# Bias rows built on all 128 partitions and stored from ScalarE's queue, recurrent blocks overlapped by one, 16 modulation chunks moved into the attention stage

## What is computed

```python
mod = silu(c) @ w_ada + b_ada                 # 6 x 1024: sh1, sc1, ga1, sh2, sc2, ga2
xn = rms_norm(h, g_mix) * (1 + sc1) + sh1
q, k, v, qi, ki, wi, xr, yr, gate_a, gate_b = split(xn @ w_in + b_in)

# attention: of each row the 128 best by the index score, a bias by distance
score = sum_h wi_h * relu(qi_h . ki); sel = top_k(causal(score), 128)
attn = softmax(q . k[sel] / 8 + rel_bias[t5_bucket(t - sel)]) @ v[sel]

# recurrent branch, 8 blocks of 128 channels
xr = causal_dwconv(xr, conv_w, conv_b)        # 4 taps
r, i = sigmoid(xr @ w_rg + b_rg), sigmoid(xr @ w_ig + b_ig)
log_a = -8 * r * softplus(-lam); a = exp(log_a)
u = xr * i * sqrt(-expm1(2 * log_a))
rnn = scan(h_t = a_t * h_{t-1} + u_t) * gelu(yr)

merged = sigmoid(gate_a) * (attn @ w_o_attn) + sigmoid(gate_b) * (rnn @ w_o_rnn)
h = h + ga1 * (merged @ w_out)                # then a gated FFN with sh2, sc2, ga2
```

## Time and profile before

| | us |
|---|---|
| median of 3 runs | 1988.12 |
| lowest, highest | 1985.82, 1991.65 |
| the profiled execution's own time | 1989.59 |
| span of its trace | 1987.5 |
| mean granted TensorE clock | 0.961 of full speed |
| PE busy | 1828.1 (92%) |
| POOL, DVE, ACT busy | 1277.8, 959.8, 660.6 |

### The profile page before, as it was taken

The page is one execution under the profiler, slowest core; times in us unless marked ns, Lnnn a source line. Parts: engine busy times, 40 slices in busy tenths (PEclk is TensorE's granted clock), DMA queues, the critical chain, the costliest instruction groups (busy, mean ns, idle before and its releaser), DMA issues.

```text
span 1987.5 us, 30490 instructions
## 1 busy us (share of the span) xinstructions
PE 1828.1 (92%) x10268; PEld 1544.2 (78%) x10268; DVE 959.8 (48%) x1524; ACT 660.6 (33%) x885; POOL 1277.8 (64%) x1685
## 2 busy tenths in 40 slices
PE   5974888899998999999889999999999989999997
PEld 2753666556776888877689999999999979998875
DVE  6743766543745444421265565456555343333211
ACT  3123565322104444410334334334433143333101
POOL 2734666325975777778656566557566757777785
PEclk8987999799999999999999999999999999999999
DMA  7644222112632333333212222222222223323332
GB/s 286 229 64 118 73 79 69 43 43 74 212 110 70 95 95 95 95 95 106 84 54 74 66 70 71 63 75 75 68 71 75 75 75 94 93 88 94 102 99 95
DMA packets 54292, 184.44 MB, mean 93 GB/s; under 512 B 6697, under 2 KB 7849, under 8 KB 54218
## 3 DMA queue, kind: packets, MB, share of 16 engines
q1 hardware_dynamic: 53066, 182.30, 30.1%
q10 hardware_dynamic: 1152, 1.05, 0.2%
HBM read 178.61 MB, written 4.72 MB: 92 GB/s over the span
## 4 chain that ended last, share of the span: by engine, by line
PE 70%; POOL 7%; DVE 7%; issue 3%; another core or an unknown queue 3%; DVEq 3%; ACT 3%; ACTq 2%; DMA 2%; SPq 1%; POOLq 0%
PE gp L383 21%; PE gp L384 21%; PE gp L385 20%; POOL Wlo L374 5%; PE A L661 3%; POOL Whi L371 2%; DVE nt L1013 1%; PE A L509 1%; PE gp L554 1%; DMA AW<-ada 1%; POOL probe L370 1%; DVE rnn_xc L1198 1%; DVE rnn_r L1211 1%; DVEq L1021 1%
## 5 line engine op out<-in xcount | busy, mean ns | idle before, releaser
L374 POOL TENSOR_TENSOR Wlo<-raw,Whi 128x256 fp32r<-128x256 f32 x1120 | 910.1, 844 | 23.4
L383 PE MATMUL gp<-XNhi,Whi 128*128 128x264 f32 (+2 forms) x2384 | 798.4, 335 | 93.9 <-DVE XNlo L1024 39.9
L384 PE MATMUL gp<-XNlo,Whi 128*128 128x264 f32 (+2 forms) x2384 | 782.7, 328 | 0.0
L385 PE MATMUL gp<-XNhi,Wlo 128*128 128x264 f32 (+2 forms) x2384 | 778.4, 327 | 0.0
L383 PEld LDWEIGHTS gp<-XNhi,Whi 128*128 128x128 f32 x2384 | 456.6, 192 | 157.9 <-POOL Wlo L374 57.4
L370 POOL TENSOR_TENSOR probe<-raw 1x1 f32<-1x1 f32 x280 | 83.7, 299 | 667.0 <-PE gp L385 595.7
L384 PEld LDWEIGHTS gp<-XNlo,Whi 128*128 128x128 f32 x2384 | 456.7, 192 | 40.5 <-issue 3.5
L385 PEld LDWEIGHTS gp<-XNhi,Wlo 128*128 128x128 f32 x2384 | 455.7, 191 | 38.6
L371 POOL TENSOR_SCALAR Whi<-raw 128x1024 fp32r<-128x1024 f32 x280 | 292.5, 1045 | 0.0
L383 PE MATMUL gp<-AChi,Whi 128*128 128x512 f32 x352 | 139.2, 396 | 1.8
L385 PE MATMUL gp<-AChi,Wlo 128*128 128x512 f32 x352 | 138.2, 393 | 0.0
(11 more groups left out here) (289 smaller groups left out, 2327.6 us busy)
## 6 DMA issues: line engine op xcount, KB each, us to landing
raw<-units SPq DMA_DIRECT2D x280, 512.0 KB, 3.5
AW<-ada SPq DMA_DIRECT2D x32, 512.0 KB, 7.2
AWM<-ada SPq DMA_DIRECT2D x8, 512.0 KB, 4.4
sq<-ada SPq DMA_DIRECT2D x8, 512.0 KB, 5.4
bias_rows<-RB SPq DMA_DIRECT2D x1, 2560.0 KB
H<-xT SPq DMA_DIRECT2D x1, 2048.0 KB, 8.8
BIAS<-bias_rows SPq DMA_DIRECT2D x1, 2048.0 KB, 8.5
out<-H SPq DMA_DIRECT2D x8, 256.0 KB, 2.1
```

Of the source, the lines that this page charges most:

```text
L374: ins = pool.tensor_tensor(lo[:, c:c + UNIT // 4], src[:, c:c + UNIT // 4], hi[:, c:c + UNIT // 4].bitcast(F32), ALU.subtract)
L383: pe.matmul(dst, Whi[s][:, k, :], rhi, start=start, stop=False)
L384: pe.matmul(dst, Whi[s][:, k, :], rlo, start=False, stop=False)
L385: return pe.matmul(dst, Wlo[s][:, k, :], rhi, start=False, stop=stop)
```

## The change

- **Bias.** `rel_bias` comes in with each head repeated 16 times, so the same two matmuls put the rows on all 128 partitions (16 partitions for a head). ACT's queue issues the store to DRAM, right behind `norm_stats(0)`; each partition writes its row 8 times. ACT's queue also issues the gather of `BIAS`, after the last `relu`. SP no longer waits for either.
- **Recurrent blocks.** `XC` and `GY` get a second buffer, and the loops are written out. PE issues the gate products of block `b - 1` behind unit `c = 0` of block `b`; ACT does `XR`, `XC` of `b`, then everything of the recurrence of `b - 1`, then `GY` and `RG8` of `b`; DVE does the taps of `b`, then the rest of `b - 1`. The last block's gates come after unit 34 (`V`). The gate weights `WG` of the next block are loaded as soon as the gate products are done.
- **Modulation.** The last 16 chunks are loaded by SP between the `rout` units, into two buffers of their own, and DVE reduces two of them in each attention step, between `p_ready` and `gated`, straight into `MOD`. `two_chunks`, the copy from `MOD4` and SP's wait for the end of the attention are gone; the merge's units are loaded by the plain `load_units`.

The core of the diff:

```diff
-            sp.wait_ge(rb_copied, 1)
-            sp.dma_start(scratch, RB[:, :]... .to_broadcast([NH, P, BIAS_W])).then_inc(bias_saved, 16)
-            sp.wait_ge(bias_saved, 16)
-            sp.dma_start(BIAS[:, :, :], bass.AP(scratch.tensor, ...)).then_inc(bias_in, 16)
-            load_units(U_RNN + 2, U_MRG + 4)
-            sp.wait_ge(at_done, QT)
-            ... two_chunks(0), unit_ahead(0), unit_ahead(1), two_chunks(2), unit_ahead(2) ...
+            load_units(U_RNN + 2, U_ROUT)
+            def load_ada3(m):
+                sp.wait_ge(ada_done, ADA_SLOTS + ADA_FIRST + ADA_SECOND + max(m - 1, 0))
+                sp.dma_start(AWM[m % 2][:, :], ada[ADA_FIRST + ADA_SECOND + m, :, :]).then_inc(ada3_in[m % 2], 16)
+            load_ada3(0); load_ada3(1)
+            load_unit(U_ROUT); load_unit(U_ROUT + 1)
+            for j in range(KC):
+                load_unit(U_ROUT + 2 + j)
+                if j < KC - 1:
+                    load_ada3(2 * j + 2); load_ada3(2 * j + 3)
+            load_units(U_MRG + 2, UNITS)
@@ PE
+            def gates(b):
+                pe.wait_ge(gate_in, b * 16 + 16)
+                pe.wait_ge(xc_ready, b + 2)
+                pe.wait_ge(ig_ready, b * 2 + 1)
+                ... the two products of WG and XC[b % 2] ...
+            for b in range(KC):
+                for c in range(3):
+                    ... unit(U_RNN + b * 3 + c) ...
+                    if b and c == 0:
+                        gates(b - 1)
@@ ACT
             norm_stats(0)
+            act.wait_ge(rb_copied, 1)
+            act.dma_start(scratch.rearrange("h (c j) m -> (h c) j m", j=NH), RB[:, :]...).then_inc(bias_saved, 16)
             ...
+            for b in range(KC):
+                XR <- psum(b * 3); XC[b % 2] <- XR
+                if b:
+                    recurrence(b - 1)      # sigmoids, WG load, exp, tanh, square, wait m2_ready, sqrt
+                GY[b % 2] <- psum(b * 3 + 1); RG8[b] <- psum(b * 3 + 2)
@@ DVE
+            for b in range(KC + 1):
+                if b < KC:
+                    three taps on XC[b % 2]
+                if b:
+                    take, U1, M2, take, UU, scan, times GY[(b - 1) % 2], split
@@ DVE, attention step (i, g)
                     dve.drain().then_inc(p_ready, 1)
+                    modulate(i * 4 + g * 2)
+                    modulate(i * 4 + g * 2 + 1)
```

More of the change, by code:

```diff
@@ L164, in build @@
                 NEG = [tri] + SC[1:]
+                AWM = [sb(f"AWM{s}", [P, UNIT], frame=fa) for s in range(2)]
                 m8 = sb("m8", [P, QT, 8], frame=fa)
@@ L772, in _ @@
             act.wait_ge(rb_mm, 1)
-            act.activation(RB[:, :], A45[0:NH, 0:BIAS_W], ACT.Copy).then_inc(rb_copied, 1)
+            act.activation(RB[:, :], A45[:, 0:BIAS_W], ACT.Copy).then_inc(rb_copied, 1)
             act.wait_ge(eps_ready, 1)
@@ new lines, in rv, with psum, load_gates, recurrence @@
+            def rv(b, c):
+                return vec("rnn", b * 16 + c)
+            def psum(g):
+                act.wait_ge(unit_done, U_RNN + g + 1 + 2)
+                return gp[g % 2][:, 0:S], gp_free[g % 2]
+            def load_gates(b):
+                act.wait_ge(gate_mm, b * 2 + 1)
+                act.dma_start(WG[:, :], gatew[b, :, :]).then_inc(gate_in, 16)
+            def recurrence(b):
+                act.wait_ge(gate_mm, b * 2 + 3)
+                act.wait_ge(rnn_done, b + 1)
+                act.activation(RG[:, :], A45[:, 0:512], ACT.Sigmoid, bias=rv(b, 7)).then_inc(ig_ready, 1)
+                act.activation(IG[:, :], A45[:, 512:1024], ACT.Sigmoid, bias=rv(b, 8)).then_inc(ig_ready, 1)
+                if b + 1 < KC:
+                    load_gates(b + 1)
+                act.drain()
+                act.activation(DA[:, :], RG[:, :], ACT.Exp, scale=LAM[:, 2, b:b + 1])
+                act.activation(TH[:, :], RG[:, :], ACT.Tanh, scale=LAM[:, 0, b:b + 1])
+                act.drain()
+                act.activation(A2[:, :], DA[:, :], ACT.Square).then_inc(a_ready, 1)
+                act.wait_ge(m2_ready, b + 1)
+                act.activation(MU[:, :], M2[:, :], ACT.Sqrt).then_inc(mult_ready, 1)
@@ new lines, in _ @@
+            load_gates(0)
+            for b in range(KC):
+                ps, free = psum(b * 3)
+                act.wait_ge(xc_ready, b + 1)
+                act.activation(XR[:, 3:3 + S], ps, ACT.Identity, bias=rv(b, 0)).then_inc(free, 1)
+                act.drain()
+                act.wait_ge(u1_done, max(b, 1))
+                act.activation(XC[b % 2][:, :], XR[:, 3:3 + S], ACT.Identity, bias=rv(b, 6), scale=rv(b, 5)).then_inc(conv_first, 1)
+                if b:
+                    recurrence(b - 1)
+                ps, free = psum(b * 3 + 1)
+                act.wait_ge(rnn_done, max(b, 1))
+                act.activation(GY[b % 2][:, :], ps, ACT.Gelu_apprx_tanh, bias=rv(b, 1)).then_inc(free, 1)
+                act.drain().then_inc(gelu_ready, 1)
+                ps, free = psum(b * 3 + 2)
+                act.activation(RG8[:, b, :], ps, ACT.Sigmoid, bias=vec("b_gates", b * 2 + 1)).then_inc(free, 1)
+                act.drain().then_inc(rgate_ready, 1)
@@ L857, in _ @@
                 act.drain().then_inc(proj_out, 1)
+                if c == 0:
+                    recurrence(KC - 1)
             act.wait_ge(v_mm, 1)
@@ L1575 @@
     }
[L1576 removed]
+    nc = bacc.Bacc("TRN2", target_bir_lowering=False, num_devices=1, dynamic_dma_scratch_size=1024)
     args, feed = [], {}
```

157 lines of the change are left out of this document (49 added, 108 removed).

## The result

| | before | after |
|---|---|---|
| median, us (runs) | 1988.88 (4) | 1937.22 (4) |
| lowest, highest | 1985.82, 1991.65 | 1935.47, 1939.00 |
| ratio, 95% interval | | 0.9741, 0.9721 to 0.9760 |
| profiled execution: span, granted clock | 1987.5, 0.961 | 1937.1, 0.969 |

The change saves 2.6%, 51.7 us between the medians. Most of what was missing is in the recurrent blocks.

What follows compares the result with a forecast made beforehand. PE, busy 92% of the span, was taken as the bound, so only its idle or delayed time could be won. Terms -33.3 + 2 + 0 - 4.5 = -35.8 gave 1952 us, range 1943 to 1960, 8 in 10 1937 to 1968.

Steps and rivals of the forecast that it cites:

- Bias, the stall: Units 11 to 12: with store and gather on ACT's queue, PE runs unit 12 at 148.6, not 174.18, 25.6 us earlier.
- Start: Before unit 0: the store's packets take turns with those of the `w_ada` chunks, +2 us, bounds 0 and about +10.
- The bound of +10 for slow packets: Start, upper bound: if store packets stay as slow as before, chunks and unit 0's weights are delayed, about +10 us.
- Recurrent blocks: Unit 12 to first logits: period 20.9 us against 23.1, set by the chain through `GY`; 7.7 us gained beyond the stall.
- from below PE alone: Recurrent blocks, lower bound of the period: 72 passes at 0.232 plus 2.4 for gate products, 19.1 us.
- Attention: Attention steps: DVE's 16 reductions fit where it waits for PE's `rout` unit, cost 0; without this cover 19.5 us.
- Merge: Merge: reductions, their loads and SP's wait go, and PE's waits for POOL shrink: -4.5 us, between -2 and -6.
- the period under 19.6: Recurrent blocks: sign that the prediction is wrong, a period under 19.6 us or over 22.
- PE-bound blocks: Rival, recurrent blocks: taps and `M2` beside quiet POOL, `GY` done before PE asks, period 19.1, total 1939 us; chance 0.12.
- The longer chain: Rival, recurrent blocks: the ACT/DVE chain stays longer, period 22 to 23, total 1960 to 1967 us; chance 0.17.
- the drain of 1.38 us: Rival, ACT's table switches in recurrent blocks: each drain adds 1.38, 2.8 per period, 19.3 more, total 1971 us; chance 0.01.
- the clock rose instead of falling: Rival "Slower", recurrent blocks: PE's idle 1.9 per block drops the clock to 1.2 GHz, up to 2071 us; chance 0.02.

Runs made afterwards that it cites:

- the late store: The kernel after, with ACT's store of the bias rows issued behind `norm_apply(0)` instead of ahead of it: 1933.40 us, ratio 0.9731.

## Why the prediction was right, and where it was off

- **Bias, the stall (-25.6):** right. The bias part alone measured -23.5 for -25.6 + 2; the store and the gather on ACT's queue hold up nothing.
- **Start (+2):** right at unit 0 (+2.2), by the mechanism given (packets one to one, the last chunk 1.2 us later). How much of it is left at unit 10 a single trace can't tell (135.8 in the kernel after, 137.8 with the bias part alone, 135.6 before); over the kernels unit 10 starts at 135.3 to 136.5 with the old start (three, mean 135.8), 133.9 to 137.8 with the new one (six, mean 136.0) and 133.5 to 134.7 with the late store (four, mean 134.2). Against the first nothing is left, against the last 1.8 us are; this stays open. The bound of +10 for slow packets was too low and in the wrong place: with the rows on 8 partitions unit 0 starts at 42.9, and it is unit 10 that is 20 us late.
- **Recurrent blocks (-7.7):** the term that was mis-sized; it measured -26.6 in the stretch from unit 12. The path was the right one, since PE does wait for ACT's `GY` once per block. The failed step is "**Then** ACT: table load 1.28, root 0.6, table load 1.28, `GY` 0.7, which ends at 15.3": the first of these loads isn't behind `M2` but ahead of it, under a wait that ACT has anyway. That is 1.28 of the 2.1 us by which `GY` is early (13.2 after t0, the start of the gate products, instead of 15.3), and putting the load back gave 1.3 more per period (20.16 against 18.84). The other 0.7 is DVE's: taps 3.3 instead of 3.9 and `M2` at its end 10.6 after t0 instead of 11.3. `GY` then ends when PE has just become free (13.0), so that the wait that was put at "some 1.9" costs 0.42 (18.84 against 18.42 without it), and the period is short by 7 x 2.06 = 14.4 us. It even lies under 19.1, the bound "from below PE alone". That bound was too high: it took 2.4 for the gate products from the earlier trace rows, where the granted clock was 0.80 on the mean, and at full clock they take 1.88. The remaining 4.4 are behind the last gate products (293.16): `M2` starts 6.6 us later and not 7.5, and from `M2` to the first logits it takes 9.5 us instead of the 13.0 of the earlier trace rows (scan 1.59 instead of 2.06, the three masks 0.89 instead of 2.95). In the trace of before POOL splits weights through nearly all of that stretch, in the kernel after it is idle from 305.2 on. The scan is the finer case: in both traces it takes 2.06 to 2.12 where half of it lies beside the `Whi` split and half beside `Wlo`, 1.59 to 1.61 beside `Wlo` alone or in part, and 1.22 in the one block of the kernel before where next to nothing lies beside it. I had carried a contended duration into a stretch that has little contention.
- **Attention (0):** right; the cover is shown by taking it away. The stretch is 1.6 us longer in the profiled execution after (97.4 against 95.8), but between kernels that do the same in it it varies from 92.9 to 97.4, with the granted clock (0.96 in the shortest, 0.92 in the longest). The mean of the eight kernels with the reductions behind `p_ready` is 94.6, that of the five without reductions there 94.4.
- **Merge (-4.5):** -3.0, within -2 to -6.
- **What no term had:** +2.1 in the FFN and the second layer (4.0 between the means of the kernels with and without the modulation part), and some of it in the merge too (0.6 in the output product), from the place of the tiles. Nothing in the prediction asked what a removed tile moves. Without it the time would have been some 4 us lower still.
- **The signs named ahead:** the stall, SP's wait, the reductions of 1.2 us, the gate products without a wait and unit 0 under 3 us late came as written; so did PE's wait for `GY` once per block, but at 0.4 us instead of 2. The first logits at 309 instead of 329 miss what was named as right, and the period under 19.6 is one that was named as wrong.
- **The rivals:** *PE-bound blocks* (0.12, 1939) is what happened but for the last 0.4 us of a block, and by another cause than its condition: the taps did lie beside POOL's split. The chance was too low because the trace of before was silent on what decides it, the place of a table load behind a wait. The load that it shows behind a long wait has its wait carried by an instruction ahead of the load. The wait for `M2` is carried by the root, with the load ahead of it, in the built program of before too, but there ACT comes to it late and the trace shows no wait. The longer chain didn't come, the drain of 1.38 us that the Trainium skill gives (ScalarE: Activation LUTs, section What ACT_TABLE_LOAD costs) is not seen (gelu starts 0.02 us behind its load, at 228.98 + 1.28 and 230.28), and the clock rose instead of falling.

## What to carry to other kernels

Before you cost a chain with table switches, find in the trace whether a load stands ahead of its activation's wait or behind it, and draw the block once for each: 1.28 us per block, 10.3 in all, hung on it here. Take durations for a moved step from rows with the same company, and look at what becomes idle beside it. When a change adds or removes tiles, look at where the operands of the large products now begin, and try a pad to 64 bytes: a removed tile of 16 bytes took back more than the edit that removed it had won, in products that nobody had touched.

## What was not expected of the hardware

- A 128x512 fp32r pass whose moving operand begins 32 bytes off a multiple of 64 starts after 233.2 to 233.3 ns on average in the down products and the first layer's output product, and after 228.9 to 229.5 where it begins at one; the granted clock is 1.00 in both. Over the kernel this is some 4 us. Other products don't follow it alone (231.7 ns on tiles that always begin at such a multiple), and why it is so is not shown by these runs.
- The store from 8 partitions kept at most 8 of the 16 engines busy in the stretch read, at 0.38 us for a packet of 2.5 KB against 0.10 from 128 partitions, and from ACT's queue it delayed the loads on SP's: unit 10 was 20 us late.
- An ACT table load for an activation that carries a wait itself runs ahead of that wait (224.39 for 228.33). With a drain between the wait and the activation it ran behind (230.10).
